# Cached sample attention in groups of four batches on column quarters of TensorE, with its loads and the group combination re-ordered

## The reference

```python
def dilated_attn_cached(q, k, v, kv_cache, window, dilation):
    k_all = concatenate([kv_cache[:, :, 0], k], axis=1)   # and v_all
    idx = n_cached + arange(T)[:, None] - dilation * arange(reach + 1)[None, :]
    s = einsum('bthd,btjhd->bhtj', q, k_all[:, idx]) * dh ** -0.5   # masked where idx < 0
    e = exp(s - max(s)); den = sum(e)
    return einsum('bhtj,btjhd->bthd', e / den, v_all[:, idx]), max(s) + log(den)
...
wts = softmax(stack(lses), axis=0)            # over the three groups
y_a = einsum('gbsh,gbshd->bshd', wts, stack(outs)) @ w_up_a
```

## Time and profile before

| what | us |
|---|---|
| median of 3 runs (2853.65 to 2867.3) | 2854.91 |
| the profiled execution | 2858.99 |
| its span, first to last instruction | 2857.2 |
| PE busy in the span | 2695.8 |
| start of the sample stage (first L1011) | 1713.7 |
| start of UP (first L699 on `mx_hi`) | 1834.6 |

### The profile page before, as it was taken

The page is one execution under the profiler, slowest core; times in us unless marked ns, Lnnn a source line. Parts: engine busy times, 40 slices in busy tenths (PEclk is TensorE's granted clock), DMA queues, the critical chain, the costliest instruction groups (busy, mean ns, idle before and its releaser), DMA issues.

```text
span 2857.2 us, 41678 instructions
## 1 busy us (share of the span) xinstructions
PE 2695.8 (94%) x16252; PEld 2586.1 (91%) x16252; DVE 978.3 (34%) x2070; ACT 400.8 (14%) x837; POOL 1041.7 (36%) x1588
## 2 busy tenths in 40 slices
PE   6899999999989999999988879889899999999997
PEld 5899999999989999999977663589899999999997
DVE  7322222222274100341016655462722222222226
ACT  4100000000030011001114431111200000000002
POOL 5444444444444444444300004005544444444440
PEclk9999999999999999999988878899999999999998
DMA  4111111111103422223134336541111111111101
GB/s 153 45 45 44 44 44 44 44 44 44 44 30 108 145 92 92 92 92 122 48 113 140 116 112 266 190 158 60 45 45 45 44 44 44 44 44 44 44 0 63
DMA packets 86150, 219.81 MB, mean 77 GB/s; under 512 B 10948, under 2 KB 64636, under 8 KB 71068
## 3 DMA queue, kind: packets, MB, share of 16 engines
q1 hardware_dynamic: 61416, 188.80, 19.4%
q10 hardware_dynamic: 24628, 29.50, 2.9%
HBM read 172.38 MB, written 45.89 MB: 76 GB/s over the span
## 4 chain that ended last, share of the span: by engine, by line
PE 83%; issue 7%; DVE 5%; DMA 2%; ACT 1%; SPq 1%; POOL 1%; DVEq 0%; POOLq 0%; ACTq 0%
PE ps L726 17%; PE ps L730 17%; PE ps L729 17%; PE ps L699 8%; PE ps L702 8%; PE ps L703 8%; DVE htmp L1524 1%; DVE h_lo L1532 1%; PE ps L962 1%; DMA o_att<-ao 1%; PE ps L941 1%; POOL wlo L683 1%; DMA raw<-stream 1%; PE ps L949 0%; PE ps L1040 0%
## 5 line engine op out<-in xcount | busy, mean ns | idle before, releaser
L678 POOL TENSOR_TENSOR whi<-raw,con 128x256 fp32r<-128x256 f32 x792 | 473.0, 635 | 1732.2 <-PE ps L726 1117.6
L726 PE MATMUL ps<-h_hi,whi 128*128 128x384 f32 (+1 forms) x3072 | 1012.7, 330 | 23.3 <-POOL wlo L683 14.2
L730 PE MATMUL ps<-h_hi,wlo 128*128 128x384 f32 (+1 forms) x3072 | 1009.8, 329 | 0.6 <-issue 0.6
L729 PE MATMUL ps<-h_lo,whi 128*128 128x384 f32 (+1 forms) x3072 | 1009.8, 329 | 0.0
L726 PEld LDWEIGHTS ps<-h_hi,whi 128*128 128x128 f32 x3072 | 578.6, 188 | 28.7 <-POOL wlo L683 16.2
L729 PEld LDWEIGHTS ps<-h_lo,whi 128*128 128x128 f32 x3072 | 578.4, 188 | 0.6
L730 PEld LDWEIGHTS ps<-h_hi,wlo 128*128 128x128 f32 x3072 | 578.4, 188 | 0.0
L683 POOL TENSOR_TENSOR wlo<-raw,whi 128x256 fp32r<-128x256 f32 x792 | 574.0, 763 | 0.0
L699 PE MATMUL ps<-act_hi,whi 128*128 128x384 f32 (+1 forms) x1056 | 348.0, 330 | 14.4 <-DVE x L1554 14.4
L1563 DVE TENSOR_TENSOR ps<-silu,ps 128x384 f32<-128x384 f32 x132 | 71.3, 540 | 833.6 <-PE ps L730 561.0
L702 PE MATMUL ps<-act_lo,whi 128*128 128x384 f32 (+1 forms) x1056 | 347.0, 329 | 0.0
(11 more groups left out here) (203 smaller groups left out, 2254.7 us busy)
## 6 DMA issues: line engine op xcount, KB each, us to landing
raw<-stream SPq DMA_DIRECT2D x99, 1024.0 KB, 4.9
vc<-vc_in SPq DMA_DIRECT2D x8, 1170.0 KB, 5.6
kc<-kc_in SPq DMA_DIRECT2D x8, 1152.0 KB, 9.8
zgate<-stage ACTq DMA_DIRECT2D x16, 384.0 KB, 2.5
sgate<-zgate SPq DMA_DIRECT2D x16, 384.0 KB, 3.3
zqko<-stage ACTq DMA_DIRECT2D x12, 384.0 KB, 2.4
oc<-o_att SPq DMA_DIRECT2D x8, 396.0 KB, 6.0
va_out<-sva ACTq DMA_DIRECT2D x24, 130.0 KB, 2.1
```

Of the source, the lines that this page charges most:

```text
L678: pool.tensor_tensor(whi[:, j, cut], raw[:, j, cut], con[:, C_ONES:C_ONES + 1].to_broadcast([P, SPLIT]), ALU.mult).then_inc(hi_split, 1)
L726: mm = pe.matmul(out, w_hi, h_hi[:, k, a:a + w], start=(k == 0), stop=False)
L729: pe.matmul(out, w_hi, h_lo[:, k, a:a + w], start=False, stop=False)
L730: mm = pe.matmul(out, w_lo, h_hi[:, k, a:a + w], start=False, stop=(k == KT - 1))
```

## The change

Batches are taken in two groups q of four. The four batches of a group use rows 32j to 32j + 31 of the PSUM banks, so each product goes to its own quarter of the output partitions, in the order j = 0 to 3 for each slice of keys. Maxima, exponentials, transposes, copies and output turns are then done once per group, on 128 partitions. All 8 batches have a key buffer of their own (in `wlo`, `whi`, `raw` and the second head's region, which are idle at the time) and five of them a value buffer; batches 5 to 7 reuse the value buffers of 1 to 3. The loads move: keys of batches 0 to 3 and values of 0 to step w = 11; the sample queries and values of 1 and 2 stay at w = 27; the new keys and values of 3 go to w = 33; keys of 4 to 7 go behind `sqb_ready` and `cs_ready`. The group combination takes two blocks at a time (four passes m) in one set of buffers, with half as many, larger DVE instructions. The first up slab is loaded after the first group's scores, the next two after the second group's, and three later slabs during UP.

```diff
+            def load_groups(m):
+                for n in range(2):
+                    sp.dma_start(oc[:, n], o_att[(2 * m + n) * P:(2 * m + n + 1) * P]).then_inc(c_in, 16)
...
                     if h + 1 < H:
                         load_head(h + 1)
                     else:
-                        load_sample()
+                        load_new(sqs, qr)
+                        for b in (1, 2):
+                            load_values_s(b)
+                if w == 11:
+                    for b in range(4):
+                        load_keys_s(b)
+                    load_values_s(0)
                 if w + LEAD < NU:
                     store_outputs(w + LEAD)
...
+                        load_new(sks, kr_out)
+                        load_values_s(3)
+                        for s in range(2):
+                            sp.wait_ge(o_stored[s], 16 * len(UNITS[s::2]))
+                        load_groups(0)
...
+            sp.wait_ge(oc_read, 1)
+            load_groups(1)
+            sp.wait_ge(sample_scored, 1)
+            slab_behind(S_UP, S_UP % 3)
+            store_pair(0)
+            sp.wait_ge(sv_full, 1)
+            for b in (5, 6, 7):
+                load_values_s(b)
+            sp.wait_ge(oc_read, 2)
+            load_groups(2)
+            sp.wait_ge(sample_scored, 2)
+            for i in (1, 2):
+                slab_behind(S_UP + i, (S_UP + i) % 3)
+            store_pair(1)
...
+                    if n in (10, 12, 14):
+                        slab_behind(S_UP + 3 + n // 2 - 5, (S_UP + n // 2 - 5) % 3)
...
+                    for g in (1, 2):
+                        for j in range(4):
+                            b = 4 * q + j
+                            mm = pe.matmul(ps[rows_of[j], g, :], sqb[:, g, p, b, :], kc[b][:, p, 512 * g - 384:512 * g + 128],
+                                           start=False, stop=last)
...
             s_scores(0)
-            for b in range(NB):
-                if b > 0:
-                    s_values(b - 1)
-                s_turn(b)
-                if b > 0:
-                    s_out_turn(b - 1)
-                if b + 1 < NB:
-                    s_scores(b + 1)
-                c_turn(b)
-            s_values(NB - 1)
-            s_out_turn(NB - 1)
+            c_turn(0)
+            s_turn(0)
+            s_scores(1)
+            s_values(0)
+            c_turn(1)
+            s_turn(1)
+            s_out_turn(0)
+            c_turn(2)
+            s_values(1)
+            s_out_turn(1)
+            c_turn(3)
...
+            combine(0)
+            s_max(0)
+            c_out(0)
+            s_turned(0)
+            combine(1)
+            s_max(1)
+            s_outputs(0)
+            for k in range(4):
                 branch_low(0, k)
+            s_turned(1)
+            c_out(1)
+            s_out(0)
+            combine(2)
+            s_outputs(1)
+            c_out(2)
+            s_out(1)
+            combine(3)
+            c_out(3)
+            for k in (4, 5):
+                branch_low(0, k)
```

More of the change, by code:

```diff
@@ L297, in program @@
         blk_ready = sem("blk_ready")
-        c_in = [sem(f"c_in{i}") for i in range(2)]
-        mix_stored = [sem(f"mix_stored{i}") for i in range(2)]
+        c_in = sem("c_in")
+        mix_stored = sem("mix_stored")
         con_in = sem("con_in")
@@ L369, in program @@
         s_const = sem("s_const")
-        s_in = [sem(f"s_in{i}") for i in range(3)]
-        sv_in = [sem(f"sv_in{i}") for i in range(2)]
+        s_in = [sem(f"s_in{b}") for b in range(NB)]
+        sv_in = [sem(f"sv_in{b}") for b in range(NB)]
         sample_stored = sem("sample_stored")
@@ L1012, in s_scores @@
+                rows_of = [slice(SROW * j, SROW * j + SROW) for j in range(4)]
+                for j in range(4):
+                    pe.wait_ge(s_in[4 * q + j], 16)
                 for p in range(2):
                     last = p == 1
-                    pe.matmul(ps[0:SROW, 0, 0:128], sqb[:, 0, p, b, :], kc[b % 3][:, p, 0:128], start=False, stop=False)
+                    for j in range(4):
+                        b = 4 * q + j
+                        pe.matmul(ps[rows_of[j], 0, 0:128], sqb[:, 0, p, b, :], kc[b][:, p, 0:128], start=False, stop=False)
@@ L1015, in s_scores @@
                     for g in range(G):
-                        pe.matmul(ps[0:SROW, 0, 128 + T * g:128 + T * g + T], sqb[:, g, p, b, :],
-                                  sks[:, g, p, T * b:T * b + T], start=False, stop=(last and g == G - 1))
-                    pe.matmul(ps[0:SROW, 1, :], sqb[:, 1, p, b, :], kc[b % 3][:, p, 128:640], start=False, stop=last)
-                    mm = pe.matmul(ps[0:SROW, 2, :], sqb[:, 2, p, b, :], kc[b % 3][:, p, 640:1152], start=False, stop=last)
-                mm.then_inc(sample_scored, 1)
@@ L1022, in s_turn @@
-            def s_turn(b):
-                pe.wait_ge(sp_ready, b + 1)
-                if b >= 1:
-                    pe.wait_ge(spt_ready, b)
+                        for j in range(4):
+                            b = 4 * q + j
+                            pe.matmul(ps[rows_of[j], 0, 128 + T * g:128 + T * g + T], sqb[:, g, p, b, :],
+                                      sks[:, g, p, T * b:T * b + T], start=False, stop=(last and g == G - 1))
+                    for g in (1, 2):
+                        for j in range(4):
+                            b = 4 * q + j
+                            mm = pe.matmul(ps[rows_of[j], g, :], sqb[:, g, p, b, :], kc[b][:, p, 512 * g - 384:512 * g + 128],
+                                           start=False, stop=last)
```

339 lines of the change are left out of this document (174 added, 165 removed).

## The result

| kernel | median of its runs, us | lowest to highest | ratio to before, 95% interval |
|---|---|---|---|
| before (4 runs beside it) | 2856.78 | 2853.65 to 2867.30 | |
| after (4 runs) | 2818.87 | 2813.68 to 2820.58 | 0.9864, 0.9842 to 0.9887 |

The forecast was 2809 in a range of 2793 to 2834, with 0.82 for faster by over 0.5%. The kernel is 1.36% faster, inside the range and 9.9 us above the point.

A forecast was written before the change was run, and what follows sets the result against it. PE was taken to set the pace, its sample-stage products filling 32 of 128 output partitions. Terms: +10.5 before the stage, -57 in it, +1 in UP, sum -45.5 from 2854.9, rounded to 2809 us; range 2793 to 2834.

The forecast's parts named there:

- the stage: Sample stage, from first scores to UP: 64 us instead of 120.9, -57 us, bounds -63 and -48.
- the full overlap: Sample stage: four quarters of output partitions run in the time of one; main case, 2809 us, chance 0.68.
- the rival without overlap: Sample stage: products on the four quarters run one by one; 2858 us, chance 0.12.
- two by two: Sample stage: quarters overlap only in twos; UP starts at 77 us, 2822 us in all, chance 0.14.
- bare weight loads: Sample stage: no overlap and 352 weight loads lie bare, 41 us more; 2899 us, chance 0.06.
- Its inside: Sample stage step by step: second scores end at 22.9 us, first values 27.5, second slab 41, POOL's splits 63.5.
- w = 11: Early key and value loads ahead of unit 14's store: 14.0 us needed, 3.5 free, so +10.5 us, bounds +5 and +14.
- w = 27: Store behind the sample loads: 12 issues fewer ahead of it, -5 us, bounds -6 and -3.
- w = 33: New-key and mask loads go in here, sample_queries waits for all: +5 us, bounds +4 and +8.
- UP: Three slab loads come between UP's gate loads: +1 us, between 0 and 6.4.
- The sign that no new stall comes at units 11 to 15: UP in the profile after: the slab loads between gates should cause no new stall at these units.

The follow-up runs named there:

- e1: After with the five loads of w = 11 moved, one each behind the stores of steps 19 to 23: 2801.68 us, ratio 0.9815.
- e3: After with the twelve new-key loads at step 33 on a semaphore of their own, which only PE's scores wait for: 2817.93 us, ratio 0.9863.
- e5: After with the third pair's group outputs and second up slab loaded ahead of values 5 to 7: 2812.03 us, ratio 0.9849.
- e6: After with the edits of e1, e3 and e5 together, no pause of POOL: 2801.09 us, ratio 0.9804.
- e8: e6 with POOL's third-slab split pausing until DVE has the last combination's minima and differences: 2798.98 us, ratio 0.9792.
- e10: e6 with the two minima of a combination written as one reduction with one SBUF input: 2795.60 us, ratio 0.9798.
- e11: e8 with POOL's pause held until the last combination's sums are through: 2797.74 us, ratio 0.9798.
- e7: e1 with POOL's third-slab split pausing until DVE has the last combination's minima and differences: 2800.75 us, ratio 0.9794.
- e9: e1 with the two minima of a combination written as one reduction with one SBUF input: 2809.71 us, ratio 0.9831.

## Why the prediction was right, and where it missed

- **What bounds the kernel, and the stage.** Right. PE's products on 32 of 128 outputs were the waste, and four quarters run in nearly the time of one; -57.9 us for -57. The choice of the full overlap from two row halves, a step beyond what the rows showed, held; the shared input partitions, which spoke for the rival without overlap, cost next to nothing (4.18 us for 4.13 on the values). The rival that no overlap comes fell with the 1.95 us of eight slices, two by two as well (2 x 1.76 = 3.5 would be its time), and bare weight loads with 7.7 us of loads that hold their engine for 2.3.
  - The Trainium skill, "TensorE: Matmul & The Clock Gate", Part 3, gives 2.38 times for three column tiles. Here it is 7.04 / 1.95 = 3.6 times for four, 0.90 of full overlap, where the page's figure, divided by three, is 0.79. Its rule that a weight load overlaps a running product only where the row group differs does not hold in this trace, and the measurement decides: all quarters use all 128 rows, and the loads overlap.
- **Its inside.** Scores were 5 us quicker than counted (the second ones end 18.0 us into the stage instead of 22.9, the first values at 22.5 instead of 27.5), because the lower clock, counted with 2.5 us in each of the two score passes, cost 0.7 us on the first slices of the first pass (2.69 against 1.95) and nothing on the slices of the second (1.95 and 1.96). That did not reach the end: from the end of the first values to the second slab it took 15.4 us instead of 13.5 (382 GB/s, where 412 was reckoned), and POOL's two slabs 25.1 instead of 22.5, as POOL takes turns with DVE. POOL was last, 2.7 us behind `mx_lo` (1791.23), where 2 was forecast. So that the stage came out within 0.5 us of its 63.5 is in part luck: errors of -5.0, +1.9 and +2.6 us cancel.
- **w = 11.** The mechanism was right, the term too small: +10.5 forecast, +13.6 in the profiled execution, within the bounds of 5 to 14, 121.6 - 109.9 = +11.7 on the mean of four kernels. A part is a wrong reading: the profile's 1152 and 1170 KB are units of 1024 bytes, so the five loads are 5.92 MB and not 5.78, and need 14.4 us, which makes the term +10.9. It showed not as one wait of about 14 us at one copy but as 9.51 and 8.41 at two, since the store of the unit before, 14, also stood behind the loads.
- **w = 27 and w = 33.** -4.5 for -5 and +3.7 for +5. The masks' wait is 5.09 us instead of 1.48, +3.6 where some 5 were forecast, and the new keys were what it waited for.
- **UP.** +0.4 for +1, but not as forecast. The sign that no new stall comes at units 11 to 15 failed: DVE waited 1.77 and 1.04 us for the gates of units 11 and 15, where it did not wait in before, and PE stood idle 1.05 us behind the first of them. On the other side, the first gate came 4.3 us into UP instead of 7.6, and PE no longer stood 1.21 us behind it; the 3.22 us of the earlier trace rows, at unit 3, became 2.59.
- **The 9.9 us to the point.** The terms of the change, all rows but the first, sum to -44.6 measured and -45.5 forecast. The other 9 are not its doing: 3.7 arose ahead of its first step, 4.1 was subtracted because the profiled execution of before lay so far above its median of three (medians of later runs of before are 2856.4 to 2857.5, so half of that was not to be had), 0.8 separates after's profiled execution from its median, and 0.4 is rounding.
- **What the prediction did not have:** what the place of the early loads was worth: 12.9 us in the stretch to unit 17 (means 121.6 and 108.7), 17.2 between the medians of after and of the later loads, 9.2 with the one-input minimum on them. It priced their cost, and did not ask whether they had to stand there.

## What to carry to other kernels

Products with few outputs gain most on column quarters if the instruction order alternates between the quarters: the same products batch by batch were 30 us slower. A load that is issued early is free only if no store that someone waits for is queued behind it; price it by the bytes ahead of that store, and look for a later place. When a stage loses its main work, list what is late next engine by engine, and where DVE and POOL both read two operands from SBUF, do not count their times as if each ran alone.

## What the runs showed of the hardware

- **A row of POOL's splits can hold a DVE instruction to its end.** Usually they take turns: next to POOL, DVE's sums of 528 elements take 1.00 us instead of 0.71, and POOL's upper part 7.07 instead of 4.60. But in seven kernels (e1, e3, e5, e6, e8, e10, e11) the first DVE instruction with two SBUF inputs that came 1.3 to 5.2 us after the third slab's first split was held until POOL was through or paused, up to 8.79 us. In three others (after, e7, e9) it came 0.2 to 0.95 us after that split and took turns. DVE's copies out of PSUM (0.68 and 0.28 us) and the reduction (0.20) passed all the while. The moment of arrival alone does not decide: with the groups first (e5) the first minimum of the combination before the last came at 1753.31, 11.45 us after the first slab's first split and 1.7 us after DVE's last instruction with two SBUF inputs, and took 0.26 us. What does decide was not tested and stays open.
  - The Trainium skill, "SBUF — State Buffer", Who interferes with whom, says that a DVE instruction with two SBUF inputs contends with a GpSimd instruction that reads SBUF and that a reduction never does. The trace agrees: 5.03 against 0.20 us in one kernel (e10).
- **Neighbouring batches overlap at their border even batch by batch.** There a batch's scores take 2.56 us from one to the next (1731.58 to 1734.14), less than its four slices of 0.88 one by one: the second half of one batch runs beside the first half of the next, on another quarter, and out of the queue's order.
